# Index masks chosen inside the stick-breaking steps instead of behind the index products

## The chip, the core and the metric

The kernel runs on one core of a Trainium2 chip. The metric is the device time of one execution in microseconds. The engines named below are TensorE (PE in the rows), VectorE (DVE), ScalarE (ACT), GpSimd (POOL) and SyncE (SP), which issues the weight loads. Each engine takes its instructions in the order of the program; semaphores make one wait for another.

## The reference, cut to what matters

The program is a transformer block with two attentions and an expert layer, followed by a second block. Only the two attentions of the first block matter here. The first ("DSA") lets each query attend to its 128 best keys by an index score; the second ("stick-breaking") has no such choice:

```python
topk = min(TOPK_MAX, s // 4)                       # 128 of 512 keys
rel = jax.nn.relu(jnp.einsum('bthd,bsd->bths', qib, ki))
score = jnp.einsum('bths,bth->bts', rel, wib).astype(jnp.float32) * idx_scale
score = jnp.where(causal[None], score, -jnp.inf)
top_score, idx = lax.top_k(score, topk)            # DSA: only these keys are attended to

z = jnp.einsum('bthd,bshd->bhts', qb, k).astype(jnp.float32) * (dh ** -0.5)
log_beta = jax.nn.log_sigmoid(z)                   # stick-breaking
log_one_minus = jnp.where(strict, log_beta - z, 0.0)
suffix = lax.cumsum(log_one_minus, axis=3, reverse=True) - log_one_minus
a = jnp.where(strict, jnp.exp(log_beta + suffix), 0.0).astype(v.dtype)
```

## The kernel before, in words

The 512 tokens are four tiles of 128. Each engine's program is written out by hand, one after another, so the order of its instructions is the order of the code. The part that matters is a chain of three stages between the first dense products and the DSA attention.

**Index stage.** For query tiles i = 1, 2, 3 TensorE makes eight small products, one for each index head (line 802), 128(i+1) keys wide, into two PSUM banks in turn. ScalarE takes each with a ReLU into one of two SBUF buffers `relu` (line 1430). VectorE adds it, weighted, to `score[i]` (a multiplication on line 2078 for the first head, then `stt`, whose instructions carry the helper's line 1948) and counts `relu_used`, which frees the buffer. Behind the eight products of a query tile TensorE computes one quarter of the value projection, `v_pair` (96 matmuls, lines 708 to 710), which ScalarE copies out (line 1421) before its next ReLU. A fourth `v_pair` ends the stage. VectorE also splits the weight tiles of `v_pair` (`low`, line 1970).

**Masks.** Behind the eight heads of a query tile VectorE calls `masks(i)`: it scales the scores (line 2060), adds the causal mask (line 2062), and then does 16 rounds of two instructions that depend on each other: `max` finds the eight largest of each row (line 2065, MAX8), `match_replace` overwrites them by the constant `TAKEN` (line 2067, MATCH_VALUE_LOAD and MATCH_REPLACE8). What is `TAKEN` at the end is the choice, and line 2069 makes `mask[i]` of it. Only the DSA attention, behind the next stage, reads the masks.

**Pair steps.** The stick-breaking attention runs in 16 steps, four head pairs p of four key tiles i = 3, 2, 1, 0 (`i = TT - 1 - step % TT`). In a step:

- TensorE makes `z_pair(step + 2)` (line 816), then `sums(step)` (line 816 again, then the sums over later key tiles on line 835, one half for each head e of the pair), then `weighted(step - 1)` (line 847). `sums` waits for GpSimd's select (line 1903), and this for VectorE's `softplus`. The sums of i = 0 are the longest and those of i = 3 the shortest.
- ScalarE takes |z|, its exponential and logarithm for step + 2 (lines 1443, 1445, 1450), and, between, the weights of step (line 1459), which wait for `mask_out`.
- VectorE does `softplus(step + 1)` (line 1948), then `mask_out(step, 0)` and `mask_out(step, 1)` (line 2110), which wait for the two halves of `sums(step)`. In steps 5, 9 and 13 it then does `take_pair` (lines 2004 and 2006), which empties PSUM bank 7 of the head pair before. TensorE's `weighted` of the next pair's first step (steps 4, 8, 12) writes to that bank and waits for it (`yb_taken`); since TensorE works in order, `sums` of steps 6, 10 and 14 stand behind it.

After the last step VectorE takes the last pair out (the fourth `take_pair`), and the DSA attention starts. From there on nothing in the program is touched.

Of the kernel before, what the change touches and what calls it, by code (L numbers as in the profile page):

```python
# [4 lines left out]
P = 128  # L5
# [3 lines left out]
TT = T // P  # L9
META = 16  # L10
L2 = META + T
NH, DH = 8, 64
HP = NH // 2
TOPK = 128
# [6 lines left out]
GATED, TAKEN = -1e30, -3e38  # L21
# [8 lines left out]
IDX_SCALE = 64 ** -0.5 * 8 ** -0.5  # L30
# [222 lines left out]
def program(nc, xT, metaT, cond, w_ada, small, onehot, rel_bias, w_stream, sub_keys, experts, outT, last_out):  # L253
    f32, u32, f32r = mybir.dt.float32, mybir.dt.uint32, mybir.dt.float32r
    ALU, ACT, AX = mybir.AluOpType, mybir.ActivationFunctionType, mybir.AxisListType.X
# [4 lines left out]
    with ctx:  # L260
        def sb(name, shape, dtype=f32):
            return ctx.enter_context(nc.sbuf_tensor(name, shape, dtype))
# [38 lines left out]
        causal = sb("causal", [P, P])  # L301
# [3 lines left out]
        col = sb("col", [P, 16])  # L305
# [6 lines left out]
        def take(*shape):  # L312
            n = 1
            for s in shape:
                n *= s
            a = arena[:, used[0]:used[0] + n]
            used[0] += n
            assert used[0] <= ARENA, used[0]
            if len(shape) == 2:
                a = a.rearrange("p (a b) -> p a b", b=shape[1])  # L320
            if len(shape) == 3:
                a = a.rearrange("p (a b c) -> p a b c", b=shape[1], c=shape[2])
            return a
# [22 lines left out]
        mask = [take(P * (i + 1)) for i in range(TT)]  # L346
# [20 lines left out]
        score = [None] + [take(P * (i + 1)) for i in range(1, TT)]  # L367
# [8 lines left out]
        def sp_of(p, i):  # L376
            return early[i][p % 2] if i >= 2 else late[i]
# [81 lines left out]
        def bank(b, width=512, start=0):  # L459
            return psum[:, b * 512 + start:b * 512 + start + width]  # L460
# [7 lines left out]
        def wait_full(eng, g, *name):  # L468

            if g and name[0] in ("in", "v", "pool"):  # L470
                at = LAST_ORDER.index({"in": IN_ORDER[1][name[1]], "v": B_V + 3, "pool": B_POOL}[name[0]])
                eng.wait_ge(tile_done.sem, tile_done.ready(FIRST_BLOCK + BLOCK + at))
            elif name[0] in BY_TILE:
                first, each = BY_TILE[name[0]]
                eng.wait_ge(tile_done.sem, tile_done.ready(FIRST_BLOCK + g * BLOCK + first + each * name[1]))
            elif name[0] == "y":
                eng.wait_ge(values_done.sem, values_done.ready(16 * g + 4 * name[1] + 3))
            else:
                for b, _, n in claimed(g, *name):
                    eng.wait_ge(bank_full[b], n + 1)  # L480
            return bank_of(g, *name)
# [8 lines left out]
        def z_both(step):  # L490
            i = TT - 1 - step % TT
            return psum[:, z_bank(step) * 512:(z_bank(step) + 2) * 512].rearrange("p (e c) -> p e c", e=2)[:, :, 0:T - P * i]

        def u_bank(step, e):
            return 4 + (2 * step + e) % 3
# [15 lines left out]
        def signal(engine, name):  # L511
            s = Signal(sem(name))
            signals[engine].append(s)
            return s
# [18 lines left out]
        relu_used = signal("dve", "relu_used")  # L533
# [826 lines left out]
        def _(act):  # L1360
# [222 lines left out]
            def block2(g):  # L1583
# [140 lines left out]
                def exponents(u):  # L1724
                    i = 2 * g + u % 2
                    keys_to = META + P * (i + 1)
                    act.wait_ge(top_ready.sem, top_ready.ready(g * 16 + u))
                    if g:
                        p = prob[u % 2][:, 0:keys_to]
                        op(p, p, ACT.Exp, scale=-1.0, bias=col[:, u % 2:u % 2 + 1],  # L1730
                           accum_out=col[:, 2 + u % 2:3 + u % 2]).then_inc(prob_exp.sem, 1)
                        return
                    b = full("scores", u)
                    steps(op(prob[u % 2][:, 0:keys_to], psum[:, b * 512:b * 512 + keys_to], ACT.Exp,
                             bias=col[:, u % 2:u % 2 + 1], accum_out=col[:, 2 + u % 2:3 + u % 2]))
                    steps.wait()
                    act.sem_inc(prob_exp.sem, 1)
                    for c, _, _ in claimed(g, "scores", u):
                        act.sem_inc(bank_free[c], 1)
# [194 lines left out]
        def _(dve):  # L1934
            V = nc.vector
            start(dve, "dve")
            steps = Steps(dve, own["dve"])
# [9 lines left out]
            def stt(out, a, s, b, op0, op1):  # L1947
                return V.scalar_tensor_tensor(out=out, in0=a, scalar=s, in1=b, op0=op0, op1=op1)  # L1948
# [18 lines left out]
            def low(n):  # L1967

                dve.wait_ge(w_rounded.sem, w_rounded.ready(n))
                V.tensor_tensor(ring_low[:, n % SLOTS, :], ring[:, n % SLOTS, :], rounded(n).bitcast(f32), ALU.subtract)\  # L1970
                    .then_inc(w_split.sem, 1)
# [81 lines left out]
            dve.wait_ge(wi_turned.sem, wi_turned.ready(0))  # L2053
            steps(V.tensor_copy(wi[:], bank(6, TT * NH).rearrange("p (a b) -> p a b", b=NH)))
            steps.wait()
            def masks(i):

                w = P * (i + 1)
                dve.wait_ge(relu_used.sem, relu_used.ready((i - 1) * NH + NH - 1))
                steps(V.tensor_scalar(score[i], score[i], IDX_SCALE, None, ALU.mult))  # L2060
                steps.wait()
                steps(V.tensor_tensor(score[i][:, w - P:w], score[i][:, w - P:w], causal[:], ALU.add))
                steps.wait()
                for r in range(TOPK // 8):
                    steps(V.max(col[:, 0:8], score[i]))  # L2065
                    steps.wait()
                    steps(V.match_replace(score[i], col[:, 0:8], score[i], TAKEN))  # L2067
                    steps.wait()
                steps(V.tensor_scalar(mask[i], score[i], 0.5 * TAKEN, -GATED, ALU.is_gt, ALU.mult))
                steps.wait()  # L2070

            n = 0
            for i in range(1, TT):
                w = P * (i + 1)
                for h in range(NH):
                    dve.wait_ge(relu_done.sem, relu_done.ready(n))
                    if h == 0:
                        ins = V.tensor_scalar(score[i], relu[n % 2][:, 0:w], wi[:, i, h:h + 1], None, ALU.mult)
                    else:
                        dve.wait_ge(relu_used.sem, relu_used.ready(n - 1))  # L2080
                        ins = stt(score[i], relu[n % 2][:, 0:w], wi[:, i, h:h + 1], score[i], ALU.mult, ALU.add)
                    ins.then_inc(relu_used.sem, 1)
                    n += 1
                if i >= 2:
                    low(S_V + 2 * i)
                    low(S_V + 2 * i + 1)
                masks(i)

            def softplus(step):
                p, i = step // TT, TT - 1 - step % TT  # L2090
                last_read = (p - 2 if i >= 2 else p - 1) * TT + TT - 1
                dve.wait_ge(soft_done.sem, soft_done.ready(step))
                if last_read >= 0:
                    dve.wait_ge(u_done.sem, u_done.ready(2 * last_read + 1))
                stt(sp_of(p, i), z_both(step), 0.0, az[i], ALU.max, ALU.add).then_inc(sp_done.sem, 1)

            def take_pair(q):
                dve.wait_ge(yb_done.sem, yb_done.ready(2 * (q * TT + TT - 1) + 1))
                low_part(y_low[1][:, q, :], bank(7), y_high[1][:, q, :])
                tell(dve, steps, yb_taken)  # L2100
# [6 lines left out]
            def mask_out(step, e):  # L2107
                dve.wait_ge(u_done.sem, u_done.ready(2 * step + e))
                u = bank(u_bank(step, e), P)
                V.tensor_tensor(u, u, strict[:], ALU.add).then_inc(u_masked.sem, 1)  # L2110

            softplus(0)
            for step in range(HP * TT):
                if step + 1 < HP * TT:
                    softplus(step + 1)
                mask_out(step, 0)
                mask_out(step, 1)
                if step < 2:
                    low(S_GATE + step)
                if step > TT and step % TT == 1:  # L2120
                    take_pair(step // TT - 1)
# [4 lines left out]
            for s in range(-1, S + 1):  # L2126
                q, i = (s + 1) // TT, (s + 1) % TT
                w = P * (i + 1)
# [470 lines left out]
```

## Time and profile before

| | us |
|---|---|
| median of 3 runs | 2430.89 (2428.23 to 2431.64) |
| the profiled execution | 2427.47 |
| its span | 2425.6 |
| TensorE busy | 1864.4 |
| VectorE busy | 1435.7 |
| ScalarE busy | 987.8 |

The span is the time between the first and the last instruction that the profiler saw; all start times in the rows count from its beginning. The stages described above lie between 166 and 345 us. A figure in square brackets behind a row of the timeline is the time that the engine was idle before it, with what ended the idle time. The granted clock (PEclk) is that of TensorE: 1.00 stands for 2.4 GHz and 0.50 for 1.2 GHz.

### The profile page before, as it was taken

The page shows a single profiled execution, that of the slowest core. Times are in us where ns is not written, and L with a number is a line of the kernel's source. Part 1 is how long each engine was busy: PE and PEld are TensorE (multiplying, and loading weights), DVE is VectorE, ACT ScalarE, POOL GpSimd, SP SyncE. Part 2 cuts the span into 40 slices and gives each one's busy share as a digit, 9 for nine tenths or more (in the row PEclk, how much of TensorE's full clock was granted, in tenths as well). Part 3 has the DMA queues.
Part 4 walks back from the last instruction along what each step waited for, and adds up shares of the span by engine and source line. Part 5 has one row for each costly group of instructions (what it writes and reads, how often), then busy time and mean ns, then how long its engine had stood idle before and what let it go on. Part 6 is the DMA issues. An engine that isn't in the chain of part 4 may idle for free.

```text
span 2425.6 us, 37910 instructions
## 1 busy us (share of the span) xinstructions
PE 1864.4 (77%) x14752; PEld 1170.2 (48%) x14752; DVE 1435.7 (59%) x3268; ACT 987.8 (41%) x2352; POOL 643.0 (27%) x554
## 2 busy tenths in 40 slices
PE   5997889999676654444444698988888885999999
PEld 3876657776433310100001352355665553677887
DVE  6758534465776677777777868775344433223554
ACT  3122545523434333333333576844444212343443
POOL 0000000000444455555555433443333331000000
PEclk8997999999877755555555797688999997999999
DMA  8921102232999999999999999999999997313655
GB/s 299 331 93 36 35 18 68 64 113 67 392 419 419 420 418 416 421 415 419 416 414 411 402 418 393 414 405 419 418 417 418 417 418 291 115 53 110 185 179 168
DMA packets 123616, 712.12 MB, mean 294 GB/s; under 512 B 14592, under 2 KB 15744, under 8 KB 57648
## 3 DMA queue, kind: packets, MB, share of 16 engines
q0 software_dynamic: 74608, 542.25, 54.2%
q1 hardware_dynamic: 48592, 167.33, 19.9%
q8 instruction: 114, 1.87, 0.3%
q14 instruction: 62, 0.51, 0.1%
q10 hardware_dynamic: 240, 0.16, 0.0%
HBM read 707.56 MB, written 2.13 MB: 293 GB/s over the span
## 4 chain that ended last, share of the span: by engine, by line
PE 46%; DMA 32%; DVE 9%; ACT 7%; POOL 3%; issue 3%; ACTq 0%; SPq 0%; DVEq 0%
DMA arena<-experts,eidx 31%; PE psum L708 8%; PE psum L709 7%; PE psum L710 7%; PE psum L1004 6%; DVE arena L1951 4%; POOL arena L1921 3%; PE psum L1295 2%; PE psum L1122 2%; PE psum L835 1%; ACT sq L1575 1%; ACT arena L1567 1%; PE psum L1317 1%; DVE arena L2067 1%; DVE col L2065 1%
## 5 line engine op out<-in xcount | busy, mean ns | idle before, releaser
L1951 DVE CUSTOM_DVE_ANT_0 arena<-arena 128x1024 f32<-128x1024 f32 x560 | 680.0, 1223 | 413.9 <-DMA arena<-experts,eidx 383.2
L1921 POOL DMA_INDIRECT arena<-experts,eidx x512 | 629.7, 1230 | 884.1 <-PE psum L1004 709.1
L1004 PE MATMUL psum<-arena,sq 32*32 32x512 f32 x8192 | 416.1, 849 | 475.0 <-ACT sq L1575 459.5
L1004 PEld LDWEIGHTS psum<-arena,sq 32*32 32x32 f32 x8192 | 68.3, 121 | 716.4 <-ACT sq L1575 672.0
L1561 ACT ACTIVATE arena<-arena 128x2 f32<-128x2 f32 x256 | 52.0, 203 | 732.7 <-DVE arena L1951 731.5
L708 PE MATMUL psum<-hn_high,w_high 128*128 128x512 f32 (+1 forms) x432 | 182.3, 422 | 16.3 <-DVE hn_low L1948 15.3
L709 PE MATMUL psum<-hn_low,w_high 128*128 128x512 f32 (+1 forms) x432 | 176.8, 409 | 0.0
L710 PE MATMUL psum<-hn_high,ring_low 128*128 128x512 f32 (+1 forms) x432 | 175.2, 406 | 0.0
L1317 PE MATMUL psum<-n_t,ring 128*128 128x256 f32 x704 | 165.4, 390 | 0.6 <-DVE n_t L1948 0.6
L1317 PEld LDWEIGHTS psum<-n_t,ring 128*128 128x128 f32 x704 | 133.3, 194 | 48.5 <-issue 30.2
L1575 ACT ACTIVATE sq<-sq,arena 128x32 f32<-128x32 f32 x512 | 136.5, 313 | 24.1 <-ACT arena L1567 0.4
L1970 DVE TENSOR_TENSOR ring_low<-ring,w_high 128x1024 fp32r<-128x1024 f32 x74 | 90.4, 1224 | 83.7 <-ACT w_high L1381 82.1
L2281 DVE TENSOR_TENSOR ring_low<-ring,last_high 128x1024 fp32r<-128x1024 f32 x66 | 80.8, 1225 | 84.0 <-ACT last_high L1599 83.2
L1381 ACT ACTIVATE w_high<-ring 128x1024 fp32r<-128x1024 f32 x74 | 77.5, 1052 | 125.0 <-PE psum L710 125.0
L1567 ACT ACTIVATE arena<-arena 128x1 f32<-128x1 f32 x512 | 122.8, 287 | 10.3
L708 PEld LDWEIGHTS psum<-hn_high,w_high 128*128 128x128 f32 (+1 forms) x432 | 84.0, 194 | 62.8 <-issue 25.7
L1599 ACT ACTIVATE last_high<-ring 128x1024 fp32r<-128x1024 f32 x66 | 69.9, 1060 | 83.1 <-DMA ring<-w_stream 83.1
L1561 ACT ACT_TABLE_LOAD x75 | 96.2, 1283 | 6.3 <-ACT hn_rest L1834 4.0
L710 PEld LDWEIGHTS psum<-hn_high,ring_low 128*128 128x128 f32 (+1 forms) x432 | 84.1, 195 | 20.9
L709 PEld LDWEIGHTS psum<-hn_low,w_high 128*128 128x128 f32 (+1 forms) x432 | 84.4, 195 | 18.3
L1903 POOL TENSOR_SCALAR_AFFINE_SELECT arena<-arena 128x256 f32<-128x256 f32 x16 | 6.5, 406 | 255.5 <-DVE arena L1948 255.5
L708 PE MATMUL psum<-last_high,n_high 128*128 128x512 f32 (+1 forms) x192 | 72.6, 378 | 1.2 <-DVE n_low L2294 1.1
(318 smaller groups left out, 3168.1 us busy)
## 6 DMA issues: line engine op xcount, KB each, us to landing
ring<-w_stream SPq DMA_DIRECT2D x262, 512.0 KB, 4.3
arena<-w_ada SPq DMA_DIRECT2D x48, 512.0 KB, 6.2
arena<-experts,eidx POOLq DMA_INDIRECT x512, 13.1
arena<-cum_rows POOLq DMA_DIRECT2D x1, 2112.0 KB, 9.8
x<-xT SPq DMA_DIRECT2D x1, 2048.0 KB, 12.7
arena<-rel_rows POOLq DMA_DIRECT2D x1, 2048.0 KB, 15.0
arena<-sub_keys POOLq DMA_DIRECT2D x1, 1024.0 KB, 5.7
outT<-hn_rest SPq DMA_DIRECT2D x8, 128.0 KB, 9.2
```

The costliest lines, as they stand in the source:

```text
L708: mm(out, a[0], b[0], start=start, stop=False)
L709: mm(out, a[0], b[1], start=False, stop=False)
L710: return mm(out, a[1], b[0], start=False, stop=stop)
L1004: last = mm(bank(4 + 2 * odd + a)[QUART * b:QUART * b + QUART, :], diag[k, s, :], rows[k, s, D + a * 512:D + (a + 1) * 512], start=c == 0, ...
L1317: last = mm(bank(b, PAIR), w[:, k, :], n_t[:, k, 0:PAIR], start=k == 0, stop=k == KT - 1)
L1561: steps(op(pre[:, s:s + 2], pre[:, s:s + 2], ACT.Gelu))
L1567: steps(op(coef[:, s + c:s + c + 1], pre[:, s + c:s + c + 1], ACT.Copy, scale=wgt[:, n // P % 2, k:k + 1]))
L1575: op(diag[:, s + c, :], ident_quart, ACT.Copy, scale=coef[:, s + c:s + c + 1]).then_inc(diag_done.sem, 1)
L1921: nc.gpsimd.indirect_dma_start(rows[:, s, :], None, experts, bass.IndirectOffsetOnAxis(ap=eidx[:, n // P % 2, n % P:n % P + 1], axis=0)).t ...
L1951: return V.tensor_tensor_reduce(out=out, in0=a, in1=b, scale=1.0, scalar=0.0 if op1 == ALU.add else -TAKEN, op0=op0, op1=op1, accum_out=accum)
L1970: V.tensor_tensor(ring_low[:, n % SLOTS, :], ring[:, n % SLOTS, :], rounded(n).bitcast(f32), ALU.subtract)\
L2281: V.tensor_tensor(ring_low[:, n % SLOTS, :], ring[:, n % SLOTS, :], last_high[:, n % SLOTS, :].bitcast(f32), ALU.subtract).then_inc(w_spli ...
```

## The change

`masks` becomes a generator that goes through all three query tiles, and gives back control after every round of `max` and `match_replace`. It isn't called in the index stage any more. Each of the 16 pair steps calls it three times, and each first step of a head pair (steps 0, 4, 8, 12) four times, behind its two `mask_out` and ahead of everything else that VectorE does in the step (`low`, `take_pair`). The 48 rounds are used up in step 14, whose third call makes the last mask.

```diff
-            def masks(i):
-
-                w = P * (i + 1)
-                dve.wait_ge(relu_used.sem, relu_used.ready((i - 1) * NH + NH - 1))
-                ...
                 if i >= 2:
                     low(S_V + 2 * i)
                     low(S_V + 2 * i + 1)
-                masks(i)
...
+            def masks():
+
+                for i in range(1, TT):
+                    w = P * (i + 1)
+                    dve.wait_ge(relu_used.sem, relu_used.ready((i - 1) * NH + NH - 1))
+                    steps(V.tensor_scalar(score[i], score[i], IDX_SCALE, None, ALU.mult))
+                    steps.wait()
+                    steps(V.tensor_tensor(score[i][:, w - P:w], score[i][:, w - P:w], causal[:], ALU.add))
+                    steps.wait()
+                    for r in range(TOPK // 8):
+                        steps(V.max(col[:, 0:8], score[i]))
+                        steps.wait()
+                        steps(V.match_replace(score[i], col[:, 0:8], score[i], TAKEN))
+                        steps.wait()
+                        yield
+                    steps(V.tensor_scalar(mask[i], score[i], 0.5 * TAKEN, -GATED, ALU.is_gt, ALU.mult))
+                    steps.wait()
+
+            choose_keys = masks()
             softplus(0)
             for step in range(HP * TT):
                 if step + 1 < HP * TT:
                     softplus(step + 1)
                 mask_out(step, 0)
                 mask_out(step, 1)
+                for _ in range(3 + (step % TT == 0)):
+                    next(choose_keys, None)
                 if step < 2:
                     low(S_GATE + step)
                 if step > TT and step % TT == 1:
                     take_pair(step // TT - 1)
```

Only VectorE's order changes. The first place is VectorE in the index stage, behind the heads of query tile 1. Before, the mask's rounds stand there (`col` holds the eight maxima, `arena` the scores):

```order
L2078 TENSOR_SCALAR arena<-arena 128x256
L1948 SCALAR_TENSOR_TENSOR arena<-arena 128x256 x7
L2060 TENSOR_SCALAR arena<-arena 128x256
L2062 TENSOR_TENSOR arena<-arena,causal 128x128
L2065 MAX col<-arena 128x8
L2067 MATCH_REPLACE arena<-col,arena 128x256
L2065 MAX col<-arena 128x8
L2067 MATCH_REPLACE arena<-col,arena 128x256
```

After the change the heads of tiles 1, 2 and 3 follow each other, and behind them the first two `softplus`:

```order
L2062 TENSOR_SCALAR arena<-arena 128x256
L1948 SCALAR_TENSOR_TENSOR arena<-arena 128x256 x7
L2062 TENSOR_SCALAR arena<-arena 128x384
L1948 SCALAR_TENSOR_TENSOR arena<-arena 128x384 x7
L1970 TENSOR_TENSOR ring_low<-ring,w_high 128x1024 x2
L2062 TENSOR_SCALAR arena<-arena 128x512
L1948 SCALAR_TENSOR_TENSOR arena<-arena 128x512 x7
L1970 TENSOR_TENSOR ring_low<-ring,v_high 128x1024 x2
L1948 SCALAR_TENSOR_TENSOR arena<-psum,arena 128x256
L1948 SCALAR_TENSOR_TENSOR arena<-psum,arena 128x512
```

So 32 instructions of rounds and their neighbours are gone from behind each group of heads. The second place is VectorE in step 5 of the pair steps, from `softplus(6)` (128x768) to `softplus(7)` (128x1024). Before:

```order
L1948 SCALAR_TENSOR_TENSOR arena<-psum,arena 128x768
L2110 TENSOR_TENSOR psum<-psum,strict 128x128 x2
L2004 CAST yb_high<-psum 128x512
L2006 TENSOR_TENSOR yb_low<-psum,yb_high 128x512
L1948 SCALAR_TENSOR_TENSOR arena<-psum,arena 128x1024
```

And after the change:

```order
L1948 SCALAR_TENSOR_TENSOR arena<-psum,arena 128x768
L2093 TENSOR_TENSOR psum<-psum,strict 128x128 x2
L2105 MAX col<-arena 128x8
L2107 MATCH_REPLACE arena<-col,arena 128x384
L2105 MAX col<-arena 128x8
L2107 MATCH_REPLACE arena<-col,arena 128x384
L2105 MAX col<-arena 128x8
L2107 MATCH_REPLACE arena<-col,arena 128x384
L2004 CAST yb_high<-psum 128x512
L2006 TENSOR_TENSOR yb_low<-psum,yb_high 128x512
L1948 SCALAR_TENSOR_TENSOR arena<-psum,arena 128x1024
```

Three rounds now stand between `mask_out(5, 1)` and `take_pair(0)`.

## Rows read from the trace of the kernel before

**Rows 1.** The page: busy time by engine, and the last chain by line.
```profile
PE 1864.4 (77%) x14752; PEld 1170.2 (48%) x14752; DVE 1435.7 (59%) x3268; ACT 987.8 (41%) x2352; POOL 643.0 (27%) x554
DMA arena<-experts,eidx 31%; PE psum L708 8%; PE psum L709 7%; PE psum L710 7%; PE psum L1004 6%; DVE arena L1951 4%; POOL arena L1921 3%; PE psum L1295 2%; PE psum L1122 2%; PE psum L835 1%; ACT sq L1575 1%; ACT arena L1567 1%; PE psum L1317 1%; DVE arena L2067 1%; DVE col L2065 1%
```
**Rows 2.** Stretches of the timeline: length, busy time (instructions), clock, DMA share, GB/s.
```profile
166.04:176.84 10.80, 6.59 (x24) 3.94 (x25) 8.47 (x15) 5.53 (x10) 0.00 (x0) 0.69 0.17 49
...
200.19:213.56 13.37, 13.37 (x97) 13.23 (x97) 12.39 (x28) 2.38 (x3) 0.00 (x0) 0.85 0.01 2
213.56:232.01 18.45, 8.36 (x18) 2.89 (x17) 15.31 (x35) 5.09 (x8) 0.00 (x0) 0.62 0.18 57
232.01:256.95 24.94, 24.94 (x197) 24.46 (x196) 23.68 (x46) 4.74 (x7) 0.00 (x0) 0.94 0.13 43
...
264.62:344.68 80.06, 73.01 (x398) 44.77 (x397) 28.19 (x56) 41.20 (x73) 5.69 (x14) 0.97 0.00 1
```
**Rows 3.** VectorE's timeline, where masks of tiles 1, 2, 3 begin and end.
```profile
177.88 0.29 DVE L2060 TENSOR_SCALAR arena<-arena 128x256 f32<-128x256 f32 x1
...
194.61 0.42 DVE L2078 TENSOR_SCALAR arena<-arena 128x384 f32<-128x384 f32 x1
...
204.04 0.35 DVE L2060 TENSOR_SCALAR arena<-arena 128x384 f32<-128x384 f32 x1
...
225.16 0.48 DVE L2078 TENSOR_SCALAR arena<-arena 128x512 f32<-128x512 f32 x1
...
235.97 0.42 DVE L2060 TENSOR_SCALAR arena<-arena 128x512 f32<-128x512 f32 x1
...
261.50 1.02 DVE L1948 SCALAR_TENSOR_TENSOR arena<-psum,arena 128x256 f32<-128x256 f32 x2
```
**Rows 4.** ScalarE's timeline: ReLUs (L1430), and the logarithm of step 1 (L1450).
```profile
190.94 0.87 ACT L1430 ACTIVATE arena<-psum 128x384 f32<-128x384 f32 x2
...
214.72 1.08 ACT L1430 ACTIVATE arena<-psum 128x512 f32<-128x512 f32 x2
225.74 0.60 ACT L1430 ACTIVATE arena<-psum 128x512 f32<-128x512 f32 x1 [9.93 <-DVE arena L2078]
...
260.13 0.63 ACT L1450 ACTIVATE arena<-arena 128x512 f32<-128x512 f32 x1
```
**Rows 5.** VectorE's groups from 264.62 to 344.68: busy, mean ns, idle before.
```profile
L1948 DVE SCALAR_TENSOR_TENSOR arena<-psum,arena 128x768 f32<-128x768 f32 (+3 forms) x14 | 12.0, 858 | 5.1 <-ACT arena L1450 4.5 <-DVE yb_low L2006 0.6
L2110 DVE TENSOR_TENSOR psum<-psum,strict 128x128 f32<-128x128 f32 x32 | 9.4, 300 | 43.7 <-PE psum L835 43.6
```
**Rows 6.** VectorE's timeline in the pair steps.
```profile
264.62 0.72 DVE L2110 TENSOR_TENSOR psum<-psum,strict 128x128 f32<-128x128 f32 x2 [2.10 <-PE psum L835]
...
279.23 0.30 DVE L2110 TENSOR_TENSOR psum<-psum,strict 128x128 f32<-128x128 f32 x1 [1.86 <-PE psum L835]
...
285.96 0.68 DVE L2004 CAST yb_high<-psum 128x512 fp32r<-128x512 f32 x1
...
290.61 0.30 DVE L2110 TENSOR_TENSOR psum<-psum,strict 128x128 f32<-128x128 f32 x1 [1.81 <-PE psum L835]
291.91 0.30 DVE L2110 TENSOR_TENSOR psum<-psum,strict 128x128 f32<-128x128 f32 x1 [1.00 <-PE psum L835]
...
343.27 0.69 DVE L2004 CAST yb_high<-psum 128x512 fp32r<-128x512 f32 x1 [4.95 <-PE psum L847]
```
**Rows 7.** TensorE's timeline: from weighted(4), and from weighted(12), to the next.
```profile
287.57 0.44 PE L847 MATMUL psum<-arena 128*64 128x128 f32 x4 [1.85 <-ACT arena L1459]
...
291.80 0.66 PE L847 MATMUL psum<-arena 128*64 128x128 f32 x8
...
326.10 0.44 PE L847 MATMUL psum<-arena 128*64 128x128 f32 x4 [1.85 <-ACT arena L1459]
...
331.75 0.66 PE L847 MATMUL psum<-arena 128*64 128x128 f32 x8
```
**Rows 8.** The stretch behind the pause of the last row pair, as in rows 2.
```profile
326.10:330.40 4.30, 4.30 (x15) 2.61 (x16) 1.22 (x1) 0.00 (x0) 0.41 (x1) 0.61 0.00 0
```

More of the change, by code:

```diff
@@ L2055, in _ @@
             steps.wait()
-            def masks(i):
-                w = P * (i + 1)
-                dve.wait_ge(relu_used.sem, relu_used.ready((i - 1) * NH + NH - 1))
[L2060 to L2070, printed above, removed]
             n = 0
```

## The prediction, written before the changed kernel ran

> **What bounds the kernel now.** I read the page first. No engine is busy throughout, and the chain that ended last is a mixture: 31% gathers of expert rows, about 22% dense products, and 1% each for the two instructions of the rounds, lines 2065 and 2067 [rows 1]. The masks are made in a stage that everything later waits for, so I went on to the stretches of that stage and to the timelines of VectorE, ScalarE and TensorE in it. The reader is to see three things.
>
> In the index stage the rounds do hold the others up, but only in part. The masks of tiles 1, 2 and 3 take 194.61 − 177.88 = 16.7, 225.16 − 204.04 = 21.1 and 261.50 − 235.97 = 25.5 us of VectorE [rows 3], 63.4 us together. Beside them TensorE works on the value projection, 13.4 us for the second quarter and 24.9 us for the last two without a gap [rows 2]. What sticks out is the pause between: from 213.56 to 232.01 TensorE is busy 8.4 of 18.5 us [rows 2].
>
> In the pair steps TensorE is the bound: busy 73.0 of 80.1 us at a granted clock of 0.97 [rows 2]. VectorE is busy 28.2 us there and waits 43.6 us for the sums of line 835 [rows 2, 5]. So there are 80.1 − 28.2 = 51.9 us of idle VectorE.
>
> And 63.4 us are to go into these 51.9. That can't be hidden, and the question is how much of the idle time can be used.
>
> **What the index stage gives back.** ScalarE's first ReLU of tile 2 is done about 191.4 (two in 190.94 to 191.81 [rows 4]), and VectorE takes it only at 194.61 [rows 3]: 3.2 us go. The first ReLU of tile 3 is done about 215.3 (214.72 + 0.6 [rows 4]), and VectorE takes it at 225.16 [rows 3]: 9.9 us go, the same wait that ScalarE shows as 9.93 us at its third ReLU [rows 4]. The products behind are paced by the ring of TensorE, ScalarE and VectorE, which the change leaves alone, so from VectorE's first multiplication to the value projection it takes as long as before. The last two quarters of the projection need only weight tiles that VectorE splits between the heads, and end 13.1 us earlier. The masks of tile 3 (25.5 us) were beside them, and TensorE gains nothing while they go.
>
> At the head of the steps the last mask ended at 261.50 and held `softplus(0)` and `softplus(1)`; `mask_out(0, 0)` started at 264.62 [rows 3, 6]. Without it `softplus(0)` is long done, and `softplus(1)` follows the logarithm of step 1, which ends at 260.13 + 0.63 = 260.76 [rows 4]. With some 0.7 us for it (the two take 1.02 us [rows 3]), `mask_out(0, 0)` can start 3.2 us earlier in relation to the projection. Sum: −16.3 us up to that instruction.
>
> TensorE's clock might give a little more. The second quarter ran at 0.85 and the last two at 0.94 [rows 2], because each started at the lower level behind a pause; all at 2.4 GHz would be 13.37 × 0.15 + 24.94 × 0.06 = 3.5 us less. But in the products of tile 1, where VectorE holds nothing up, the clock fell as well (0.69 from 166.04 to 176.84 [rows 2]). I take 0, with −3.5 as the other end.
>
> **What the pair steps pay.** From `mask_out(0, 0)` to the end of the fourth `take_pair` before: 80.06 us. After, VectorE has its 28.2 us and the 63.4 us of masks, 91.6 us, and what it still waits. Step by step:
>
> - In most steps nothing. `softplus(step + 1)` stands ahead of the rounds, so GpSimd and TensorE make the next sums while VectorE does its rounds (three of about 1.0 us for tile 1, 1.3 us for tile 2, 1.6 us for tile 3: the masks' times over 16), and `mask_out` finds them done.
> - In the four steps of i = 0 the second half of the sums comes 1.86 us behind the first [rows 6], and no round stands between the two `mask_out`: 4 × 1.86 = 7.4 us.
> - In steps 5, 9 and 13 the rounds stand ahead of `take_pair`. TensorE's `weighted(4)` waits for it, and `sums(6)` stands behind. Before, `take_pair(0)` started at 285.96, right behind `mask_out`, and TensorE's pause was 1.85 us [rows 6, 7]. Now three rounds (3.9 us) are ahead of it, and VectorE has come late to the step already by the four calls of step 4. TensorE's pause becomes some 9 to 10 us (3 us of rounds of step 4 after its sums are done, `softplus` and two `mask_out` 1.5 us, 3.9 us, `take_pair` 1.4 us). Behind it VectorE has nothing but `softplus(7)` until TensorE has made the first half of `sums(6)`: it waits 1.81 us and 1.00 us as before [rows 6], and none of it is filled. 3 × 2.8 = 8.4 us.
> - At the end the wait for `weighted(15)` is as before, 4.95 us [rows 6], and 0.6 us stand ahead of three `softplus` [rows 5].
>
> That is 21.4 us of waits, and 91.6 + 21.4 = 113.0 us in place of 80.1: +32.9 us.
>
> **The clock.** Behind a pause of 1.85 us, TensorE ran part of the steps' work at 1.2 GHz: the granted clock from 326.10 to 330.40 is 0.61 [rows 8]. The same stretch of work, from `weighted` to the next, took 291.80 − 287.57 = 4.23 us at 2.4 GHz and 331.75 − 326.10 = 5.65 us there, and it had a product of about 0.3 us less to do [rows 7]: 1.7 us lost. Behind pauses of 9 us, three in number, it will certainly start at 1.2 GHz, and VectorE waits for just this work. All of it at half speed would cost 4.2 us. Bounds 3 × 1.7 and 3 × 4.2; I take 2.5 each, nearer to the row: +7.5 us.
> The Trainium skill, "TensorE: Matmul & The Clock Gate", section "HAM oscillation — how this bites in real kernels", says that a loop whose bursts of matmuls are parted by long pauses starts each burst at the lower clock, and pays for it anew every time. The trace agrees for the pause before 232.01, and the row of 326.10 shows it even behind a short one; by this page the second bound applies, and the change would be 5 us worse than my sum.
>
> **The sum.** −16.3 + 32.9 + 7.5 = +24.1 us. Behind the steps the DSA attention, the dense products and the gathers follow in a row, with nothing that could start without the steps, so the shift goes through. The profiled execution took 2427.47 us and would take 2451.6. The median of the runs is 3.4 us above it (2430.89), which gives 2455.0.
>
> **Rivals.**
>
> 1. *TensorE's clock isn't touched.* For it: three pauses of 1.85 us stood in the steps before, and the clock was 0.97 over all. Against: [rows 8], and pauses five times as long. −16.3 + 32.9 and up to −3.5: 2444 to 2447.5.
> 2. *The lower clock stays for most of the steps.* TensorE now has 73 us of work in 113 us. Then the halves of the i = 0 sums part by 3.7 instead of 1.86 us (+7.4), the first halves come later than the rounds (some +10), and the other waits double (+13 in all with the end): 30 us more, less the 7.5 already in the sum, about 2478.
> 3. *The index stage gives nothing back*, because the ring of products or the projection's loads end last in it. Against: 9.93 us of ScalarE's waiting end with VectorE's multiplication. It would be 13.1 us more: 2468.
> 4. *Faster: the rounds fall wholly into VectorE's waits.* It has 51.9 us of them, so at the least 63.4 − 51.9 = 11.5 us come on top, against 16.3 us given back: −4.8, and with the clock of the projection −8.3, so 2422.6. It decides itself at the waits that stay: under 16.3 − 11.5 = 4.8 us of them (I count 21.4) the change is no loss. For it: the step's work is spread evenly, 3 us a step against 3.2 us of idle time. Against: the order of `take_pair`, and 4.95 us at the end that no round can fill.
>
> **How the numbers follow.** The forecast has a chance of 0.62, rival 1 0.15, rival 2 0.08, rival 3 0.06, rival 4 0.09. About 0.2% (5 us) is what a measurement tells from no change. Rival 4 gives 0.07 of faster, and 0.02 of it stay within the bound; the rest, 0.91, is slower. The range reaches from below rival 1, with its gain of the projection's clock, to beyond rival 3: 2440 to 2472. It leaves out rivals 2 and 4.
>
> **What would show it.** In the profile after: from the end of the projection's second quarter to the start of its third some 8.6 us in place of 18.5; VectorE busy over 75% from there to the end of the steps; three pauses of TensorE of 8 to 10 us, each ended by line 2006 of `take_pair`, with a granted clock well under 1.00 behind; some 113 to 120 us from the first `mask_out` to the end of the fourth `take_pair`. The prediction is wrong if the steps grow by under 20 us, or if the pauses ahead of `weighted(4)`, `weighted(8)` and `weighted(12)` stay near 2 us.

## The result

The changed kernel takes 2442.67 us (median), against 2428.23 us for the kernel before in the same runs: a ratio of 1.0055 (95% interval 1.0042 to 1.0067). It is slower by 13 to 14 us, where 24 were forecast; 2442.67 lies near the lower end of the range of 2440 to 2472. One of its five runs took 2675.18 us in a slower state, at a granted clock of 0.679, and the ratio leaves it out. The same kernel on another occasion came to 1.0065 (1.0053 to 1.0077). Its profiled execution took 2442.67 us with a span of 2440.7, 15.1 us more than the span before.

The stretches that answer to [rows 2], in the changed kernel: the second quarter of the projection, the products of tile 3, the last two quarters, and the steps from the first `mask_out` to the end of the fourth `take_pair`. The busy times in such a row are those of TensorE, its weight loads, VectorE, ScalarE and GpSimd, in this order.

```profile
195.89:207.48 11.59, 11.59 (x97) 11.46 (x96) 3.61 (x5) 2.49 (x4) 0.00 (x0) 1.00 0.01 1
207.48:214.48 7.00, 5.92 (x17) 2.06 (x16) 4.22 (x6) 4.72 (x8) 0.00 (x0) 1.00 0.43 150
214.48:238.12 23.64, 23.64 (x197) 23.18 (x196) 4.22 (x6) 4.86 (x8) 0.41 (x1) 1.00 0.13 45
242.59:361.43 118.84, 82.26 (x396) 49.31 (x396) 85.92 (x210) 43.57 (x76) 6.11 (x15) 0.83 0.00 1
```

The pause of TensorE between the second and the third quarter shrank from 18.5 to 7.0 us, and the clock is 1.00 in all three rows, where it was 0.85, 0.62 and 0.94. The products themselves, from VectorE's first multiplication to the projection behind, took less time too, in tile 2 and in tile 3. Before:

```profile
194.61:200.19 5.58, 4.53 (x9) 2.00 (x9) 3.60 (x7) 2.45 (x5) 0.00 (x0) 0.50 0.00 0
225.16:232.01 6.85, 5.62 (x9) 2.00 (x9) 4.36 (x7) 2.99 (x5) 0.00 (x0) 0.50 0.00 0
```

And in the changed kernel:

```profile
191.59:195.89 4.30, 3.89 (x13) 1.77 (x13) 3.49 (x6) 2.54 (x6) 0.00 (x0) 1.00 0.58 228
209.27:214.48 5.21, 4.79 (x12) 1.76 (x12) 4.22 (x6) 3.07 (x6) 0.00 (x0) 1.00 0.45 182
```

The steps grew from 80.1 to 118.8 us, and in them the clock fell from 0.97 to 0.83. VectorE's groups in the steps, which answer to [rows 5]:

```profile
L2105 DVE MAX8 col<-arena 128x8 f32<-128x256 f32 (+2 forms) x48 | 26.8, 558 | 1.2
L2107 DVE MATCH_REPLACE8 arena<-col,arena 128x256 f32<-128x256 f32 (+2 forms) x48 | 26.0, 542 | 0.0
...
L2093 DVE TENSOR_TENSOR psum<-psum,strict 128x128 f32<-128x128 f32 x32 | 8.6, 293 | 23.6 <-PE psum L835 23.6
L2107 DVE MATCH_VALUE_LOAD arena<-col,arena 128x8 f32 x48 | 4.4, 92 | 1.7
L2004 DVE CAST yb_high<-psum 128x512 fp32r<-128x512 f32 x4 | 2.8, 691 | 5.1 <-PE psum L847 5.0
```

Of the 43.6 us that VectorE waited for TensorE's sums, 23.6 are left. TensorE's timeline shows the three pauses ahead of `weighted(4)`, `weighted(8)` and `weighted(12)`, and what follows the first of them, for [rows 7]:

```profile
277.78 0.70 PE L847 MATMUL psum<-arena 128*64 128x128 f32 x4 [9.06 <-DVEq L621]
...
284.46 0.66 PE L847 MATMUL psum<-arena 128*64 128x128 f32 x8
...
309.18 0.69 PE L847 MATMUL psum<-arena 128*64 128x128 f32 x4 [10.26 <-DVEq L621]
...
341.46 0.70 PE L847 MATMUL psum<-arena 128*64 128x128 f32 x4 [10.68 <-DVEq L621]
```

The releaser is VectorE's semaphore at the end of `take_pair` (line 621 is the helper that counts `yb_taken`). From `weighted(4)` to `weighted(5)` TensorE needs 284.46 − 277.78 = 6.68 us, in place of 4.23. Behind the other two pauses it needs 6.35 and 7.04 us (to 315.53 and 348.50). VectorE's own timeline in steps 5 and 6, which answers to [rows 6]:

```profile
276.16 0.69 DVE L2004 CAST yb_high<-psum 128x512 fp32r<-128x512 f32 x1
276.88 0.69 DVE L2006 TENSOR_TENSOR yb_low<-psum,yb_high 128x512 fp32r<-128x512 f32 x1
277.79 1.22 DVE L1948 SCALAR_TENSOR_TENSOR arena<-psum,arena 128x1024 f32<-128x1024 f32 x1 [0.21 <-DVE yb_low L2006]
283.27 0.30 DVE L2093 TENSOR_TENSOR psum<-psum,strict 128x128 f32<-128x128 f32 x1 [4.26 <-PE psum L835]
284.57 0.30 DVE L2093 TENSOR_TENSOR psum<-psum,strict 128x128 f32<-128x128 f32 x1 [1.00 <-PE psum L835]
```

Behind `take_pair` VectorE has only `softplus(7)` to do, and then waits 4.26 and 1.00 us for the sums that it held up itself.

### The profile page after: what moved, and what is told of

Same layout as the page of the kernel before. It is cut to its first block, busy times and chain, and to the rows that moved or that the text cites. A ratio compares the mean times of both kernels' runs of the same rounds, so it can differ in the third digit from the quotient of the medians.

```text
span 2440.7 us, 37917 instructions
## 1 busy us (share of the span) xinstructions
PE 1863.3 (76%) x14752; PEld 1166.7 (48%) x14752; DVE 1433.3 (59%) x3268; ACT 987.6 (40%) x2352; POOL 629.9 (26%) x554
## 4 chain that ended last, share of the span: by engine, by line
PE 46%; DMA 33%; DVE 8%; ACT 7%; POOL 3%; issue 3%; ACTq 0%; DVEq 0%; SPq 0%
DMA arena<-experts,eidx 32%; PE psum L708 8%; PE psum L709 8%; PE psum L710 8%; PE psum L1004 6%; DVE arena L1951 4%; POOL arena L1921 3%; PE psum L1295 2%; PE psum L1122 2%; PE psum L835 1%; ACT sq L1575 1%; ACT arena L1567 1%; PE psum L1210 1%; PE psum L1172 1%; DMA arena<-w_ada 1%
## 5 line engine op out<-in xcount | busy, mean ns | idle before, releaser
L1921 POOL DMA_INDIRECT arena<-experts,eidx x512 | 616.7, 1204 | 895.5 <-PE psum L1004 722.0
L1575 ACT ACTIVATE sq<-sq,arena 128x32 f32<-128x32 f32 x512 | 136.5, 313 | 24.1 <-ACT arena L1567 0.4
## 6 DMA issues: line engine op xcount, KB each, us to landing
x<-xT SPq DMA_DIRECT2D x1, 2048.0 KB, 12.6
```

The source lines that it names most:

```text
L1575: op(diag[:, s + c, :], ident_quart, ACT.Copy, scale=coef[:, s + c:s + c + 1]).then_inc(diag_done.sem, 1)
L1921: nc.gpsimd.indirect_dma_start(rows[:, s, :], None, experts, bass.IndirectOffsetOnAxis(ap=eidx[:, n // P % 2, n % P:n % P + 1], axis=0)).t ...
```

## The experiments

In each, "the steps" are the stretch from the first `mask_out` to the end of the fourth `take_pair`, and "the index stage" is the time from ScalarE's first copy of the projection to its fourth (line 1421). The kernel before has 66.97 us in the second (190.02 to 256.99), and the changed one 48.03 (190.15 to 238.18).

**e1: `take_pair` ahead of the rounds.**

```diff
-                for _ in range(3 + (step % TT == 0)):
-                    next(choose_keys, None)
-                ...
                 if step > TT and step % TT == 1:
                     take_pair(step // TT - 1)
+                for _ in range(3 + (step % TT == 0)):
+                    next(choose_keys, None)
```

> The changed kernel with one line moved: take_pair stands ahead of the rounds in steps 5, 9 and 13 instead of behind them. Theory A (the rounds cost most where they delay take_pair, because TensorE then stands still and VectorE afterwards waits with nothing to do): the rounds of these steps (3.9, 4.6 and 4.6 us) move into VectorE's waits of 3.9 to 4.3 us for the first half of the next sums, so some 12 to 13 us go: about 2430 us, ratio to before 1.000 to 1.002. Rival B (VectorE is simply full in the steps, and where its rounds stand does not matter): as the changed kernel, 2442 to 2443 us, ratio 1.0055.

Measured: 2434.52 us, ratio 1.0015 (1.0006 to 1.0024). The steps, and VectorE's timeline in step 5 and 6 of this kernel:

```profile
242.70:348.70 106.00, 84.56 (x396) 50.79 (x396) 85.73 (x210) 43.64 (x76) 6.09 (x15) 0.86 0.00 1
```
```profile
272.60 0.68 DVE L2004 CAST yb_high<-psum 128x512 fp32r<-128x512 f32 x1
...
277.32 0.54 DVE L2107 MATCH_REPLACE8 arena<-col,arena 128x384 f32<-128x384 f32 x1
277.90 1.22 DVE L1948 SCALAR_TENSOR_TENSOR arena<-psum,arena 128x1024 f32<-128x1024 f32 x1
279.80 0.30 DVE L2093 TENSOR_TENSOR psum<-psum,strict 128x128 f32<-128x128 f32 x1 [0.68 <-PE psum L835]
281.21 0.30 DVE L2093 TENSOR_TENSOR psum<-psum,strict 128x128 f32<-128x128 f32 x1 [1.11 <-PE psum L835]
```

The wait of 4.26 us is down to 0.68, since the three rounds now lie in it. The steps are 12.8 us shorter with the same work on VectorE (85.7 and 85.9 us busy). Rival B falls: some ten of the changed kernel's microseconds are the place of one call. What is left of TensorE's pause ahead of `weighted(4)` is 5.31 us in place of 9.06, and now ScalarE's weights end it, which had waited for `mask_out`:

```profile
274.20 0.69 PE L847 MATMUL psum<-arena 128*64 128x128 f32 x4 [5.31 <-ACT arena L1459]
...
281.10 0.66 PE L847 MATMUL psum<-arena 128*64 128x128 f32 x8
```

Behind it the work to the next `weighted` takes 6.90 us: a pause of 5.31 us is followed by the lower clock too (0.59 in that stretch).

**e2: no rounds at all.** The kernel before, with `range(0)` for the rounds; the choice of keys is left out.

```diff
-                for r in range(TOPK // 8):
+                for r in range(0):
```

> The kernel before, with none of the 48 rounds of max and match_replace (the choice of keys is left out; the scale, the causal mask and the mask's comparison stay). It shows what the index stage gives when the rounds are gone and the steps get nothing in their place. Theory A (two waits, the head of the steps, and TensorE's clock that stays at 2.4 GHz through the stage): 22 us less, about 2406 us, ratio 0.991; the products of tile 3 and the second quarter of the projection at the higher clock. Rival B (the waits alone, as the prediction had it): 16.3 us less, about 2412 us, ratio 0.9933. In both the steps take about 80 us as before.

Measured: 2410.71 us beside 2429.85, ratio 0.9915 (0.9901 to 0.9929), 19 to 21 us less. The interval holds theory A and leaves rival B out by a little. The profile is less kind to the theory, and its span is only 14.8 us under the one before. The index stage takes 50.77 us (191.66 to 242.43), 16.2 less than before, not 18.9 as in the changed kernel: within the small products of tile 3 the clock fell, which it had not in the changed kernel. In e2 it is 1.00 from 209.00 to 213.00 and 0.50 from 214.00 to 217.55. The stretches in this kernel: second quarter, products of tile 3, last two quarters, and the steps.

```profile
197.38:209.00 11.62, 11.62 (x98) 11.46 (x97) 4.55 (x8) 2.52 (x4) 0.00 (x0) 1.00 0.01 1
209.00:217.55 8.55, 7.67 (x17) 2.48 (x16) 4.42 (x7) 4.98 (x8) 0.00 (x0) 0.76 0.38 123
217.55:242.40 24.85, 24.84 (x197) 24.32 (x196) 5.17 (x8) 4.73 (x7) 0.41 (x1) 0.95 0.12 43
246.84:330.02 83.18, 74.60 (x396) 45.85 (x396) 28.10 (x57) 43.42 (x76) 6.10 (x15) 0.96 0.00 1
```

TensorE's work and its waits are the same as in the changed kernel up to there (the longest is 0.68 us in both); 8.55 against 7.00 us and 24.85 against 23.64 are the clock alone, 2.8 us. And the steps take 83.2 us without a round in them, 3.1 more than before.

**e3: no rounds for tile 3.** The choice for the last query tile is left out.

```diff
-                for r in range(TOPK // 8):
+                for r in range(0 if i == 3 else TOPK // 8):
```

> The kernel before without the 16 rounds of tile 3 alone (their 24 us of VectorE; the choice of keys for the last query tile is left out). Theory A: these rounds lay beside two quarters of the projection, and only their end held the first softplus up: 3.2 us less, about 2425 us, ratio 0.9987. Rival B: the index stage pays for every round alike, 25.5 of 63.4 us of masks, so 25.5/63.4 of the 22 us: 8.9 us less, about 2419 us, ratio 0.9963.

Measured: 2431.22 us beside 2429.85, ratio 1.0002 (0.9993 to 1.0012). Both expectations miss: the rounds of tile 3 cost nothing where they stood, less than theory A allowed. The first `mask_out` does come early: 260.74 − 256.32 = 4.4 us behind the fourth copy of the projection, in place of 7.6. But the steps then take as much longer:

```profile
260.74:343.92 83.18, 74.60 (x396) 45.88 (x396) 28.09 (x57) 43.45 (x76) 6.11 (x15) 0.96 0.00 1
```

83.2 us, as in e2. From the fourth copy of the projection to the end of the steps it is 87.60 us, and 87.69 in the kernel before. What VectorE does earlier at the head of the steps is given back in them, where VectorE doesn't set the pace.

**e4: extra products in the pauses of the index stage.** The kernel before; nothing is left out.

```diff
                 for h in range(NH):
+                    if h == 2 and i > 1:
+                        for _ in range((3, 9)[i - 2]):
+                            mm(bank(7), neg_ones[:], x[:, 0, META:], start=True, stop=True)
                     pe.wait_ge(relu_done.sem, relu_done.free(n, 2))
```

> The kernel before with 3 and 9 extra products (512 columns, into a bank nobody reads) that TensorE does in its two pauses ahead of the third product of tiles 2 and 3. Nothing is left out. Theory A (the 5.7 us that the index stage gave back beyond the forecast are TensorE's clock, which fell in these pauses): the second quarter of the projection takes 11.6 us in place of 13.4, the stretch from VectorE's first multiplication of tile 3 to the third quarter 5.2 in place of 6.9, granted clock near 1.00; over all only 2 to 4 us less, since VectorE's masks still stand in the chain: 2424 to 2426 us, ratio 0.9984 to 0.9992. Rival B (the clock falls because of the small products themselves, or the time came from elsewhere): stretches and time as before, ratio 1.000.

Measured: 2429.49 us beside 2429.85, ratio 0.9997 (0.9986 to 1.0007). No change that can be told. The stretches: products of tile 2 from VectorE's first multiplication, second quarter, products of tile 3, last two quarters.

```profile
194.10:199.30 5.20, 4.09 (x11) 1.57 (x10) 4.26 (x8) 2.53 (x6) 0.00 (x0) 0.80 0.01 2
199.30:213.00 13.70, 13.70 (x98) 13.57 (x98) 12.38 (x27) 2.31 (x3) 0.00 (x0) 0.83 0.01 2
224.20:229.90 5.70, 4.58 (x8) 1.38 (x8) 4.88 (x7) 2.98 (x5) 0.00 (x0) 0.83 0.00 0
229.90:255.60 25.70, 25.70 (x197) 25.28 (x196) 23.70 (x47) 4.74 (x7) 0.00 (x0) 0.91 0.12 42
```

A small part of theory A holds: the products of tile 3 took 5.7 us in place of 6.9, and those of tile 2 5.20 in place of 5.58. But the clock fell later, during the products, and the projection behind started low all the same and was no faster (13.70 and 25.70 us at 0.83 and 0.91, against 13.37 and 24.94). The index stage is 65.99 us (189.79 to 255.78), 1.0 less than before. TensorE's timeline shows that the pauses weren't filled to their ends. Ahead of the products that wait for VectorE, 1.11 and 2.30 us of 2.89 and 9.41 stayed:

```profile
195.33 3.86 PE L805 MATMUL psum<-arena 64*128 64x384 f32 x8 [1.11 <-ACT arena L1433]
...
225.32 4.74 PE L805 MATMUL psum<-arena 64*128 64x512 f32 x8 [2.30 <-ACT arena L1433]
```

The clock was still 1.00 from 223.02 to 227.40, beyond the second of them, and 0.61 from 227.40 to 229.90. So the clock didn't stay up through these products though most of each pause was filled. The run doesn't tell whether the short pauses that stayed, or the sparse products, brought it down.

**e5: extra products in the three pauses of the steps.** The changed kernel; nothing is left out.

```diff
                 pe.wait_ge(a_done.sem, a_done.ready(2 * step + 1))
+                if i == TT - 1 and p:
+                    for _ in range(9 if p == 1 else 10):
+                        mm(bank(u_bank(step + 2, 0)), neg_ones[:], x[:, 0, META:], start=True, stop=True)
```

> The changed kernel with 9, 10 and 10 extra products (512 columns, into the bank of the next sums, which overwrite them) that TensorE does while it waits for take_pair in steps 5, 9 and 13. Nothing is left out. Theory A (behind each of the three pauses the work that VectorE waits for runs at 1.2 GHz; in the changed kernel 6.7, 6.4 and 7.0 us from one weighted to the next in place of 4.2): the three stretches take 4.2, 4.2 and 4.0 us and 6 to 7.5 us go: about 2436 us, ratio 1.003. Rival B (the clock doesn't matter, VectorE's total does): 2442 to 2443 us, ratio 1.0055. If the extra products last longer than the pause, it gets slower.

Measured: 2441.0 us, ratio 1.0044 (1.0031 to 1.0058). TensorE around the first pause of this kernel, and the steps:

```profile
268.75 7.89 PE L844 MATMUL psum<-x,neg_ones 128*128 128x512 f32 x18
...
277.89 0.44 PE L850 MATMUL psum<-arena 128*64 128x128 f32 x4 [1.25 <-DVEq L621]
...
282.12 0.66 PE L850 MATMUL psum<-arena 128*64 128x128 f32 x8
```
```profile
242.69:353.84 111.15, 101.29 (x454) 57.06 (x454) 85.97 (x210) 43.57 (x76) 6.13 (x15) 0.95 0.00 1
```

From `weighted(4)` to `weighted(5)` 4.23 us, exactly as before the change, and the steps are 118.84 − 111.15 = 7.7 us shorter: what the clock cost in them, shown by the profile. The time over all moved less than theory A had it (ratio 1.003), and the two intervals overlap, so the time alone doesn't rule rival B out. The profile's first gather came 6.4 us earlier (616.3 against 622.7), while it was 3.2 us longer from there to the last one (1425.2 against 1422.0). The size of 7.7 us is shown for the steps and not for the whole kernel.

**e6: the rounds spread over VectorE's idle times.** `masks()` stands ahead of the index heads, and

```diff
+            def rounds(count):
+                for _ in range(count):
+                    next(choose_keys, None)
...
+                rounds((13, 7, 0)[i - 1])
...
+            rounds(12)
             softplus(0)
+            rounds(4)
...
                 mask_out(step, 0)
+                rounds(step % TT == 3)
                 mask_out(step, 1)
                 if step > TT and step % TT == 1:
                     take_pair(step // TT - 1)
+                rounds((0, 1, 2, 0)[step % TT])
```

> The same 48 rounds, put where the changed kernel's VectorE has nothing to do: 13 behind the heads of tile 1, 7 behind those of tile 2, 12 ahead of softplus(0) and 4 behind it, all beside the projection; the last 12 (tile 3, 1.5 us each) in the steps, one between the two mask_out of steps 3, 7 and 11, one behind take_pair in steps 1, 5 and 9, two in steps 2, 6 and 10. Theory A (a round costs only where TensorE waits for what stands behind it): the index stage keeps its 22 us, the steps pay 0 to 4 us: 2406 to 2411 us, ratio 0.991 to 0.993. Rival B (every round in the steps costs its time): 18 us more, about 2424 us, ratio 0.998. Rival C (the rounds in the index stage hold its products up again): 2415 us or more.

Measured: 2411.99 us beside 2430.75, ratio 0.992 (0.9906 to 0.9934). This is faster than both kernels, by some 19 us than the kernel before, with nothing left out. The steps:

```profile
245.90:329.00 83.10, 74.60 (x396) 45.83 (x396) 45.54 (x94) 43.34 (x76) 6.09 (x15) 0.96 0.00 1
```

83.10 us with 12 rounds in them, and 83.18 in e2 with none. The index stage is 50.78 us (190.63 to 241.41), and 50.77 in e2 with none. All 48 rounds are free. Theory A holds, and rivals B and C fall.

**e7: 13 rounds in the index stage, two or three in each step.** As e6, with `rounds((13, 0, 0)[i - 1])`, none around `softplus(0)` or between the two `mask_out`, and `rounds(2 + (step % TT == 0))` behind `take_pair`.

> 13 of the 48 rounds behind the heads of tile 1 (they fill VectorE's 13.8 us there), the other 35 in the steps, two per step and three in steps 0, 4, 8 and 12, behind take_pair. VectorE then has some 28 + 50 = 78 us of work in steps that last about 82 us without rounds. Theory A (a round is free as long as it fits into the wait that stands at its place; what doesn't fit is paid): the waits between the two mask_out of i = 0 (1.9 us, four times) and the end (5 us) stay unfilled, so the steps take 88 to 93 us and the kernel 2415 to 2421 us, ratio 0.994 to 0.9965. Rival B (only a full VectorE costs, and 78 is under 82): about 2411 us, ratio 0.992, as with the 12 rounds. Rival C (any round in the steps is paid in full): 44 us over e6's 12 less, 2440 us.

Measured: 2427.35 us beside 2429.64, ratio 0.9988 (0.9979 to 0.9997). The steps, and VectorE's wait for the sums in this kernel:

```profile
242.50:341.90 99.40, 81.75 (x396) 49.06 (x396) 73.62 (x169) 43.76 (x76) 6.11 (x15) 0.88 0.00 1
```
```profile
L2118 DVE TENSOR_TENSOR psum<-psum,strict 128x128 f32<-128x128 f32 x32 | 8.7, 294 | 19.5 <-PE psum L835 19.5
```

All three expectations miss. VectorE is busy 73.6 us of steps that last 83.2 without rounds, and still they grow by 16 us. Theory A had the direction and half of the size: it counted the waits that no round stands in, and not that rounds which end late hold `mask_out` up, and with it ScalarE's weights and TensorE. The pauses ahead of `weighted(4)`, `weighted(8)` and `weighted(12)` are 3.81, 5.53 and 4.61 us in this kernel, where they were 1.85:

```profile
272.55 0.54 PE L847 MATMUL psum<-arena 128*64 128x128 f32 x4 [3.81 <-ACT arena L1459]
...
297.11 0.69 PE L847 MATMUL psum<-arena 128*64 128x128 f32 x4 [5.53 <-ACT arena L1459]
...
322.71 0.69 PE L847 MATMUL psum<-arena 128*64 128x128 f32 x4 [4.61 <-ACT arena L1459]
```

Behind each the lower clock follows (0.71, 0.56 and 0.62 up to the next `weighted`).

**e8: the changed kernel again.**

> The changed kernel itself, on the chip and beside the runs of before that e7 has, to see how far its cost and the stretches move from one set of runs to another: where the prediction failed was a size of some 6 us in the clock. Theory A (the size was off because TensorE's clock falls in one execution at a place where it doesn't in another): the ratio lies within 1.0045 to 1.007 again, and the profile shows 48.0 or 50.8 us from the first to the fourth copy of the projection, nothing between. Rival B (the 48.0 us belong to this order of instructions): 48.0 us again, as in the three profiles of this order so far.

Measured: 2444.97 us beside 2429.64, ratio 1.0065 (1.0053 to 1.0077). The ratio lies where theory A put it, and the profile answers for rival B: 48.04 us from the first copy of the projection to the fourth (189.34 to 237.38), as in the changed kernel, e1, e5 and e7 (48.02 to 48.04), while e2 and e6 have 50.8. Five profiles against two speak against chance from one execution to the next. They don't exclude it, since e2 and e6 were profiled once each.

## Why the prediction was right in kind and wrong in size

Slower, through VectorE's rounds ahead of `take_pair`, was right. The sum was 24.1 us, and the profile shows 15.1 (the medians of the two sets 14.4 and 15.3). By its own steps:

- **The two waits of the index stage (−3.2 and −9.9).** Both went. VectorE's first multiplications now follow the ReLU at once, and the pause between the quarters is 7.0 us, even under the 8.6 foretold.
- **The head of the steps (−3.2).** Seen in the changed kernel: `mask_out(0, 0)` is 242.59 − 238.18 = 4.4 us behind the fourth copy, in place of 7.6. e2 and e3 show it given back in full in steps that VectorE doesn't bound. That it is a gain in the changed kernel, because VectorE is the bound there, is argued and was not tested.
- **TensorE's clock in the index stage (0, with −3.5 as the end). This is the step that failed.** From the first copy of the projection to the fourth it takes 18.9 us less, of which the waits are 13.1: 5.8 us are the clock, beyond even the bound of 3.5. These are most of the 9 us by which the sum missed. The text said that the products "take as long as before" and took 0 because the clock had fallen in the products of tile 1. Both inferences were wrong. The products of tiles 2 and 3, from VectorE's first multiplication to the projection, went from 5.58 and 6.85 us at a clock of 0.50 to 4.30 and 5.21 at 1.00, and the projection's quarters from 13.37 and 24.94 to 11.59 and 23.64. Tile 1 was no measure for the others. Dense work stood ahead of its products as well (1.00 from 140.00 to 165.94), but TensorE has a pause of 3.40 us within them, and from 170.00 on the clock is 0.50:

```profile
165.94:170.00 4.06, 1.76 (x13) 1.26 (x12) 3.95 (x4) 2.15 (x3) 0.00 (x0) 1.00 0.46 131
170.00:176.84 6.84, 4.93 (x12) 2.77 (x13) 4.52 (x12) 3.37 (x8) 0.00 (x0) 0.50 0.00 0
```

In tiles 2 and 3 of the changed kernel the longest pause is 0.68 us, and TensorE stayed at 2.4 GHz. e2 and e6 keep just part of it (2.8 us less), so the size is not certain even from one order of instructions to a very similar one.
- **The steps (+32.9, and +7.5 for the clock).** Forecast 120.5 us with both, measured 118.84: 1.7 less. The waits for the sums are 23.6 us, where 15.8 plus the clock's 7.5 were expected; the three pauses are 9.06, 10.26 and 10.68 us, where 9 to 10 stood. e1 shows that 12.8 us of it are the place of `take_pair`, and e5 that 7.7 us are the clock. The three stretches behind the pauses took 6.68, 6.35 and 7.04 us, in e5 4.23, 4.24 and 4.01. That is 7.6 us more, the 7.5 of the sum and not the second bound of 12.6, which would have made the change 5 us worse.
- **"The shift goes through."** Nearly. At the end of the steps the changed kernel is 361.43 − 344.68 = 16.75 us behind, and at its end 15.1. The kernel before had a low clock at the start of the DSA attention (0.77 from 344.68 to 350.00), and the changed one had not (1.00 from 361.43 to 366.75). From TensorE's first product there to the next of its kind it took 346.12 to 351.29 = 5.17 us before, and 362.86 to 366.47 = 3.61 after: these are the 1.6 us.

Together: 24.1 − 5.8 − 1.7 − 1.6 = 15.0.

One of the signs did not come: VectorE was to be busy over 75% from the start of the third quarter to the end of the steps, and it is busy 90.7 of 147.0 us, 62%.

Rival 1, that TensorE's clock isn't touched, comes nearest in number (2444 to 2447.5), but that is luck: the clock of the steps fell from 0.97 to 0.83 at a cost of 7.7 us, and the 5.8 us of the index stage, which stood at nothing in the sum, made up for most of it. Rival 2 falls with 118.84 us of steps, where it had some 30 us on top of 113, and rival 3 with the 18.9 us that the index stage gave back. Rival 4, the faster one, fell as it should: the waits that stayed are 28.6 us, and it needed them under 4.8. But its thought was sound for another order: e6 puts all rounds into VectorE's waits, and the index stage keeps the 16.2 us that it gives back in e2, without any rounds.

What stays open: why the clock holds through the products of tile 3 in the changed kernel, e1, e5, e7 and e8, and falls in e2 and e6, where TensorE's instructions are the same and its longest pause is 0.68 us too; and what brought it down in e4, the short pauses that were left or the sparse products.

## What to carry to other kernels

Work moved into an engine's idle time is free only at the places of its waits: look, call by call, who waits for what stands behind it. Against the 83.2 us that the steps take without rounds, the 48 rounds cost nothing at places picked from the timeline (e6, most of them in the index stage), 35.7 us with three or four per step ahead of the one call that frees a PSUM bank, and 22.8 us with that call put first (e1). And when a stall of TensorE goes, price the work behind it again at the clock that it will then have.

## What the runs showed of the hardware

- VectorE's busy share says little about room: in e7 the steps grew by 16 us though VectorE's work, 73.6 us, is 10 us short of the 83.2 that they take without rounds.
- Behind pauses of 9.1 to 10.7 us TensorE's work up to the next `weighted` took 6.4 to 7.0 us in place of 4.0 to 4.2, and e5 restored these by keeping TensorE busy in the pauses. Behind 5.31 us of pause in e1 it took 6.90.
- A clock that has risen can hold through sparse work: the products of tile 3 in the changed kernel keep TensorE busy 5.9 of 7.0 us at 1.00, and with 7.7 of 8.6 us busy it was 0.76 on average in e2.
